# A hybrid decoder trunk on one core: branch gates computed one half branch ahead, and ScalarE's functions grouped by table

## The chip, the core and the metric

The kernel runs on one core of one Trainium2 chip. The metric is the device time of one launch in microseconds (us), lower is better. Engines are named as in the profile: PE is TensorE, DVE is VectorE, ACT is ScalarE, POOL is GpSimd, SP is SyncE, which here only issues DMAs.

## What is computed

Two layers of a decoder trunk act on 544 tokens (T: 512 of a prompt, 32 of eight sampled sequences), model width 1024, all in float32. A layer is, cut to what matters:

```
h = rmsnorm(x); p = h @ w_in            # columns for A, B, C, D and four gates of 1024 columns each
A: sparse attention                     # exp
B: retention, per-head norm; silu(g) * o          # rsqrt as exp(-0.5 ln), silu
C: HGRN2: silu(q), sigmoid(f), sigmoid(-f), ln, exp; per-head norm; silu(g) * o
D: Mamba-2: softplus(dt), exp, silu(conv); silu(z) * y; norm
up_b = branch_b @ w_branch[b]           # b = A, B, C, D
x = x + (sum_b sigmoid(gate_b) * up_b) @ w_out
x = x + (silu(rmsnorm(x) @ w_g) * (rmsnorm(x) @ w_u)) @ w_down
```

## The kernel before, in words

The residual x and the normed h lie transposed in SBUF for the whole run (`xT`, `hT`: 8 blocks of 128 channels by 544 tokens), and so do the four branch outputs (`brT`). Everything multiplied by a big weight is a **job**: a block of 512 weight columns, loaded by SP into one of two ring slots (`stream`), so that job j waits until job j-2 is finished on PE. `table` lists the products of all jobs in PE's order. A product of a gate is 128 columns by 272 tokens, 8 matmuls, and a gate job has 8 of them; a `wb` job (one half, 512 of 1024 columns, of a branch's projection) has 8 products of 4 matmuls. The trace records each of these float32 matmuls twice.

Product k goes into PSUM bank 6 + k%2, so PE may begin product k only when product k-2 has been taken out. ACT takes the gates (`take_act`: a copy per product into `sg`, and after the eighth one sigmoid over the whole half, 128 by 2176), and DVE takes the `wb` products (`take_dve`: times the gate, then added into `mg`). There is one `sg`, so DVE's first take of a `wb` job waits for the sigmoid of the gate job right ahead of it, and the next gate's first copy waits for the last take of the `wb` job before it.

The mixers B, C and D are chains over five token tiles (four of 128 tokens, one of 32) in which PE, ACT and DVE hand small matrices to each other. To fill PE's gaps the job products are dealt out among the chain's steps: `Share` holds the last job of a stage and a weight per gap, and at each `share.point` all three engines do their part of the products up to there. Every engine runs in program order, so a gate copy on ACT stands behind the chain's functions, and a `wb` take on DVE behind the chain's vector work. The stages are `stage_a` (A, with the jobs up to `dt`), `stage_retention` (gate00, wb00, gate01, wb01; the digits are branch and half), `stage_hgrn` (gates and wb of branch 1), `stage_ssm` (branch 2, in a part for the convolution and one for the scan), `stage_merge` (branch 3, then `wo`) and `stage_ff`.

The columns that B, C and D need (jobs r0 to r3, c0 to c3, z, xbc, dt) are copied by ACT out of PSUM into `stage` and sent to the DRAM buffers `spill`; the stages read them back tile by tile (L1438 for B, L1801 for C, L1960 for z). ACT applies silu to the tile when it is in: L1320 for B, L1597 and L1598 for C, L2070 for z. In B's stage SP does, from tile 2 on, in this order for each tile i: wait for the result of tile i-2 (`b_y`), load tile i, then load the next weights:

```
for i, (t0, m) in enumerate(tiles):
    if i >= 2:
        sp.wait_ge(S("b_y"), i - 1)
    sp.dma_start(inputs[0:m, i % 2], spill[0:4, ...]).then_inc(...)
    if i == 1: (load the states)
    if i >= 2:
        stream(sp, min(job0 + i - 1, job0 + 2), l)
```

ACT holds one set of function tables at a time. Where a function is not in the set that is loaded, an ACT_TABLE_LOAD stands ahead of it. The per-tile norm is ln and then exp (L1340 and L1341 in B, L1652 and L1653 in C, L2096 and L2097 in D) and each of the two gets a load of its own.

Of the kernel before, what the change touches and what calls it, by code (L numbers as in the profile page):

```python
# [53 lines left out]
def constants():  # L54
# [64 lines left out]
    for g in range(2):  # L119
# [8 lines left out]
HALF = T // 2  # L128

LAYER_SEMS = ("proj_ready", "taken_act", "taken_dve", "weights_in0", "weights_in1", "down_job_done", "dve_step", "act_step",  # L130
              "merged", "spilled0", "spilled1", "spilled2", "spilled3", "h_ready", "next_tile_in", "ret_stored", "hgrn_stored", "ssm_stored")


def trunk(nc, inp, out):

    es = ExitStack()
    with es:
# [46 lines left out]
        spill_dt = nc.dram_tensor("spill_dt", [T, 8], F32).ap()  # L184
        ps = [es.enter_context(nc.psum_tensor(f"ps{i}", [P, 512], F32)) for i in range(8)]
# [11 lines left out]
        sg = arena[:, AN - 4 * T:AN].rearrange("p (c t) -> p c t", c=4)  # L197
        merge_tmp = arena[:, AN - 5 * T:AN - 4 * T].rearrange("p (i t) -> p i t", i=2)
# [111 lines left out]
        for row in table:  # L310
            starts.append(starts[-1] + row[4])
        def in_strips(k):

            name, natural, at, _, _, _ = table[k]
            return natural and at == NT and jobs[J[name]][2] == 512
# [44 lines left out]
        def take_act(act, k):  # L360
# [27 lines left out]
            elif name[:4] == "gate":  # L388
                ins = act.activation(sg[:, at // P, t], bank[:, 0:HALF], ACT.Copy)  # L389
                if at == 3 * P and half == 1:  # L390
                    ach.link(act, ins)
                    ins = act.activation(sg[:, :, :], sg[:, :, :], ACT.Sigmoid)  # L392
            elif name[:2] == "gu":
                ins = act.activation(sg[:, at // P, t], bank[:, 0:HALF], ACT.Silu)  # L394
            else:
# [11 lines left out]
                else:  # L407
                    row = 8 if name == "z" else int(name[1]) + (4 if name[0] == "c" else 0)
                    if in_strips(k):
                        ins = act.activation(st[:, 0:P], bank[:, 0:P], ACT.Copy)  # L410
# [13 lines left out]
        def take_dve(dve, k):  # L424
# [7 lines left out]
            if name[:2] == "wb":  # L432
                n, db = jobs[J[name]][1]
                gate = max(i for i in range(k) if table[i][0][:4] == "gate")
                dve.wait_ge(S("taken_act"), taken_by(gate)[1])
                dst = mg[:, db * 4 + at // P, t]
                if n == 0:
                    dve.tensor_tensor(dst, bank[:, 0:HALF], sg[:, at // P, t], ALU.mult).then_inc(S("taken_dve"), 1)
                else:
                    tm = merge_tmp[:, k % 2, :]  # L440
                    dve.tensor_tensor(tm, bank[:, 0:HALF], sg[:, at // P, t], ALU.mult).then_inc(S("taken_dve"), 1)  # L441
# [28 lines left out]
        def take_to(who, eng, upto):  # L470
            for k in range(done[who], upto):
                if who == "act" and (table[k][0][:4] == "gate" or table[k][0][:2] == "gu") and table[k][5] == "act":

                    last = [i for i in range(k) if table[i][5] == "dve" and
                            (table[k][0][:4] == "gate" or table[i][0][:2] == "wo" or table[i][2] - 256 == table[k][2])]
# [121 lines left out]
        def rms_act(act):  # L597
            act.wait_ge(S("sq_summed"), 1)
# [25 lines left out]
        def stage_a(l):  # L624
# [140 lines left out]
            share = Share("r3", weights)  # L765
            with nc.Block() as block:
                @block.sync
                def _(sp):
                    stream(sp, J["r3"] + 3, l)
# [467 lines left out]
        def stage_retention(l):  # L1237
# [17 lines left out]
            job0 = J["gate01"]  # L1255
            with nc.Block() as block:
# [59 lines left out]
                def _(act):  # L1316
                    def gate(i):
                        m = tiles[i][1]
                        act.wait_ge(S(f"b_tile_in{i % 2}"), 16 * (i // 2 + 1))
                        act.activation(g(i)[0:m, :], g(i)[0:m, :], ACT.Silu).then_inc(S("b_inputs"), 1)  # L1320

# [5 lines left out]

                    share.point("act", act)
                    gate(0)
                    take_turned(0)  # L1330
                    for i, (t0, m) in enumerate(tiles):
                        share.point("act", act)
                        if i < 4:
                            gate(i + 1)
# [14 lines left out]
                def _(dve):  # L1349
# [25 lines left out]
                    for i, (t0, m) in enumerate(tiles):  # L1375
# [49 lines left out]
                        dve.wait_ge(S("b_inputs"), i + 1)  # L1425
# [6 lines left out]
                def _(sp):  # L1432
                    for w in range(4):
                        sp.wait_ge(S(f"spilled{w}"), 16 * 5)
# [12 lines left out]
                    for w in range(4):  # L1447
                        sp.wait_ge(S(f"spilled{w}"), 16 * 10)
# [8 lines left out]
        def stage_hgrn(l):  # L1457
# [28 lines left out]
            job0 = J["gate11"]  # L1486
            zbank = (0, 5)
            with nc.Block() as block:
# [98 lines left out]
                def _(act):  # L1587
                    def gates(i):
# [8 lines left out]
                        act.activation(q(i)[0:m, :], q(i)[0:m, :], ACT.Silu)  # L1597
                        act.activation(g(i)[0:m, :], g(i)[0:m, :], ACT.Silu).then_inc(S("c_inputs"), 1)  # L1598
# [65 lines left out]
                def _(dve):  # L1664
# [3 lines left out]
                    def forget(i):  # L1668
# [10 lines left out]
                        dve.wait_ge(S("c_inputs"), i + 1)  # L1679
# [134 lines left out]
        def stage_ssm(l):  # L1814
# [19 lines left out]
            with nc.Block() as block:  # L1834
# [35 lines left out]
                def _(act):  # L1870
# [4 lines left out]
                    ins.then_inc(S("conv_in_taken"), 1)  # L1875
                    act.wait_ge(S("dt_abs"), 1)
# [36 lines left out]
                def _(sp):  # L1913
                    for w in range(4):
                        sp.wait_ge(S(f"spilled{w}"), 16 * (17 if w < 2 else 16))
# [37 lines left out]
            job0 = J["gate21"]  # L1953
            with nc.Block() as block:
# [106 lines left out]
                def _(act):  # L2061
                    def take_front(i):
# [261 lines left out]
```

## Time and profile before

| | |
|---|---|
| device time, median of 3 runs (lowest, highest) | 4283.37 us (4275.71, 4287.13) |
| the profiled execution: device time | 4269.23 us |
| the profiled execution: span | 4267.4 us |
| PE busy | 3759.9 us, 88% |
| DVE busy | 1501.5 us, 35% |
| ACT busy | 859.2 us, 20% |
| mean granted clock of PE | 0.928 |

The span is cut by stage in the first layer as follows (the second layer is 2102.6 us later and the same): attention and the jobs up to `dt` to 806 us, B 812 to 979, C to 1247, D's convolution to 1318, D's scan to 1485, merge and `wo` to 1643, the feed-forward part to 2150. A busy time of PE is summed over instructions whose ends are modelled; time is lost where PE idles, and where the granted clock is below 1.00 (0.50 is 1.2 GHz, 1.00 is 2.4 GHz). A row "A <- B" says that A's engine was idle until B released it.

### The profile page before, as it was taken

To read this page: it belongs to the slowest core of one execution; us is meant where nothing else is said; L and a number is where in the kernel's file an instruction comes from. 1 tells how busy PE (TensorE), PEld (TensorE's weight loads), DVE (VectorE), ACT (ScalarE), POOL (GpSimd) and SP (SyncE) were. 2 spreads that over 40 slices of the span, in tenths; PEclk is the share of its full clock that TensorE was granted. 3 is DMA by queue.
4 is the path that set the end of the run, shared out by engine and by line. 5 is a ranking of instruction groups with operands and counts; after the bars stand their busy time and mean duration, and the time that the engine had idled before them with its cause. 6 is when DMAs were issued, how large, how long until landed. Compare 5 with 4: busy or idle time off the path is not lost. (4 is left out here: it accounts for less than half of the span.)

```text
span 4267.4 us, 43291 instructions
## 1 busy us (share of the span) xinstructions
PE 3759.9 (88%) x17542; PEld 2611.1 (61%) x17542; DVE 1501.5 (35%) x2591; ACT 859.2 (20%) x1674; POOL 198.4 (5%) x214
## 2 busy tenths in 40 slices
PE   5988899888878699999988889998788777999998
PEld 2543446666646477888845344566566564878887
DVE  2146393146745411000012555813476542110000
ACT  1122222124413210000012222222244141000000
POOL 0000411100000000000000013120000000000000
PEclk9988999799979799999999889998899788999999
DMA  3210454522121111212122124443211211212121
GB/s 99 71 61 33 147 170 131 180 76 70 45 72 61 53 69 60 79 60 74 55 67 82 38 69 161 167 164 133 83 57 35 72 61 49 72 60 79 60 74 56
DMA packets 254256, 352.57 MB, mean 83 GB/s; under 512 B 38142, under 2 KB 144254, under 8 KB 253924
## 3 DMA queue, kind: packets, MB, share of 16 engines
q1 hardware_dynamic: 213948, 249.67, 17.7%
q0 software_dynamic: 21504, 75.51, 5.3%
q10 hardware_dynamic: 18600, 24.55, 1.6%
q8 instruction: 142, 2.33, 0.2%
q14 instruction: 62, 0.51, 0.0%
HBM read 306.04 MB, written 43.66 MB: 82 GB/s over the span
## 5 line engine op out<-in xcount | busy, mean ns | idle before, releaser
L354 PE MATMUL ps<-hT,ring 128*128 128x272 f32 x5632 | 1391.2, 404 | 141.6 <-ACT arena L389 72.7
L354 PEld LDWEIGHTS ps<-hT,ring 128*128 128x128 f32 x5632 | 1083.4, 196 | 409.7 <-issue 98.3
L346 PE MATMUL ps<-ring,hT 128*128 128x512 f32 (+3 forms) x1728 | 718.8, 558 | 50.9 <-ACT stage L413 24.7
L346 PEld LDWEIGHTS ps<-ring,hT 128*128 128x128 f32 (+1 forms) x1728 | 305.8, 200 | 370.1 <-issue 335.7
L354 PE MATMUL ps<-branchT,ring 128*128 128x272 f32 x1024 | 289.4, 431 | 77.0 <-DVE arena L441 31.5
L2231 PE MATMUL ps<-arena,ring 128*128 128x272 f32 x1408 | 323.7, 393 | 3.0 <-DVE xT L2249 1.9
L2231 PEld LDWEIGHTS ps<-arena,ring 128*128 128x128 f32 x1408 | 267.2, 190 | 59.5 <-issue 2.7
L354 PEld LDWEIGHTS ps<-branchT,ring 128*128 128x128 f32 x1024 | 202.5, 206 | 154.6 <-DVE arena L441 40.8
L453 DVE TENSOR_TENSOR arena<-ps,arena 128x272 f32<-128x272 f32 x88 | 38.9, 442 | 602.0 <-PE ps L354 602.0
L394 ACT ACTIVATE arena<-ps 128x272 f32<-128x272 f32 x88 | 35.0, 397 | 586.6 <-PE ps L354 586.6
L910 DVE MAX8 branchT<-arena 32x8 f32<-32x2080 f32 x64 | 148.2, 2316 | 2.2
L911 DVE MATCH_REPLACE8 arena<-branchT,arena 32x2080 f32<-32x2080 f32 x64 | 147.0, 2297 | 0.0
L2249 DVE TENSOR_TENSOR xT<-xT,ps 128x272 f32<-128x272 f32 x32 | 11.5, 429 | 320.1 <-PE ps L2231 320.1
L441 DVE TENSOR_TENSOR arena<-ps,arena 128x272 f32<-128x272 f32 x96 | 42.1, 439 | 222.2 <-ACT arena L392 166.3
L354 PE MATMUL ps<-arena,ring 128*128 128x272 f32 x512 | 117.8, 393 | 2.2 <-issue 2.2
L354 PEld LDWEIGHTS ps<-arena,ring 128*128 128x128 f32 x512 | 97.1, 190 | 22.9 <-issue 3.0
L1149 ACT ACTIVATE branchT<-ps 128x512 f32<-128x512 f32 x128 | 69.5, 594 | 194.7 <-PE ps L1054 194.4
L389 ACT ACTIVATE arena<-ps 128x272 f32<-128x272 f32 x128 | 50.0, 391 | 254.8 <-PE ps L354 254.6
L801 PE MATMUL ps<-cst,arena 128*128 128x128 f32 x160 | 35.1, 324 | 52.0 <-ACT arena L852 51.7
L852 ACT ACTIVATE arena<-arena 128x128 f32<-128x128 f32 (+3 forms) x64 | 35.9, 561 | 204.7 <-DVE arena L893 204.7
L682 DVE TENSOR_TENSOR branchT<-arena 128x2560 f32<-128x2560 f32 (+1 forms) x4 | 8.6, 2154 | 190.8 <-PEq L643 190.8
L599 ACT ACT_TABLE_LOAD x4 | 5.1, 1283 | 337.9 <-issue 178.3
(384 smaller groups left out, 3810.1 us busy)
## 6 DMA issues: line engine op xcount, KB each, us to landing
ring<-in_w_in SPq DMA_DIRECT2D x44, 2048.0 KB, 8.3
ring<-in_w_gu SPq DMA_DIRECT2D x44, 1024.0 KB, 6.3
spill<-stage ACTq DMA_DIRECT2D x72, 256.0 KB
ring<-in_w_branch SPq DMA_DIRECT2D x16, 1024.0 KB, 5.0
arena<-spill SPq DMA_DIRECT2D x16, 1024.0 KB, 5.2
ring<-in_w_down SPq DMA_DIRECT2D x8, 2048.0 KB, 7.8
ring<-in_w_out SPq DMA_DIRECT2D x4, 2048.0 KB, 7.8
ring<-in_w_down SPq DMA_DIRECT2D x4, 1536.0 KB, 6.5
```

The lines of the kernel that those rows point to most:

```text
L346: mm = pe.matmul(bank[0:m, 0:w], hT[:, c, t0:t0 + m], slot3(j)[:, c, 0:w], start=(c == 0), stop=(c == kn - 1))
L354: mm = pe.matmul(bank[:, 0:HALF], slot3(j)[:, c, at:at + P], src, start=(c == 0), stop=(c == kn - 1))
L389: ins = act.activation(sg[:, at // P, t], bank[:, 0:HALF], ACT.Copy)
L394: ins = act.activation(sg[:, at // P, t], bank[:, 0:HALF], ACT.Silu)
L441: dve.tensor_tensor(tm, bank[:, 0:HALF], sg[:, at // P, t], ALU.mult).then_inc(S("taken_dve"), 1)
L453: dve.tensor_tensor(ff_ref[0][:, n, t], bank[:, 0:HALF], sg[:, (at - 256) // P, t], ALU.mult).then_inc(S("taken_dve"), 1)
L801: mm = pe.transpose(ps[2 + n % 2][:, s * P:s * P + P], Pr[:, n % 2, s * P:s * P + P], ident)
L852: act.activation(Pr[:, n % 2, 0:L], St[:, n % 2, 0:L], ACT.Exp, bias=mx[:, n % 2, 0:1], accum_out=sm[:, n % 2, 0:1]).then_inc(S("att_probs ...
L910: vch.link(dve, dve.max(m, src))
L911: vch.link(dve, dve.match_replace(work, m, src, TAKEN))
L1149: act.activation(KT[:, bb, j, :], ps[j][:, :], ACT.Copy).then_inc(S("kt_ready"), 1)
L2231: mm = pe.matmul(ps[2 * dc + half][:, 0:HALF], w, ff[:, fc, half * HALF:half * HALF + HALF], start=(fc == 0), stop=(fc == FC - 1))
```

## The change

Gates: there are now two gate buffers. Half 0 keeps `sg`; half 1 goes into `xT[:, 4:8]`, the upper half of the residual, which is stored to DRAM at the layer's start (`saved_x`) and loaded back in `stage_merge` before `wo1`. The jobs are reordered so that the gate of a half branch stands one `wb` job ahead: gate00, gate01, wb00, gate10, wb01, gate11, wb10, gate20, wb11 and so on to gate31, wb30, wb31. A gate's first copy waits for the `wb` job that used the same buffer last.

ACT: silu is applied in the copy out of PSUM for r3, c0, c3 and z, so the stages no longer apply it; the order of the projection jobs is changed so that these four stand together. `preload_act_table_set` names a set that has both ln and exp, at the head of the stages, after each gate sigmoid and after C's sigmoids.

```diff
-        jobs += [(f"r{i}", R_Q + 512 * i, 512) for i in range(4)]
-        jobs += [(f"c{i}", C_Q + 512 * i, 512) for i in range(4)]
-        jobs += [("z", M_Z, 512), ("xbc0", M_X, 512), ("xbc1", M_X + 512, 512), ("dt", M_DT, 8)]
+        jobs += [(f"r{i}", R_Q + 512 * i, 512) for i in range(3)] + [("c2", C_Q + 1024, 512), ("r3", R_Q + 1536, 512)]
+        jobs += [("c0", C_Q, 512), ("c3", C_Q + 1536, 512), ("z", M_Z, 512), ("c1", C_Q + 512, 512)]
+        jobs += [("xbc0", M_X, 512), ("xbc1", M_X + 512, 512), ("dt", M_DT, 8)]
         for n in range(4):
             for db in range(2):
-                jobs += [(f"gate{n}{db}", GATES + n * DM + db * 512, 512), (f"wb{n}{db}", (n, db), 512)]
+                if n == 0 and db == 0:
+                    jobs += [("gate00", GATES, 512)]
+                n2, d2 = n + db, 1 - db
+                if n2 < 4:
+                    jobs += [(f"gate{n2}{d2}", GATES + n2 * DM + d2 * 512, 512)]
+                jobs += [(f"wb{n}{db}", (n, db), 512)]
...
+        gates = (sg, xT[:, 4:8, :])
...
             elif name[:4] == "gate":
-                ins = act.activation(sg[:, at // P, t], bank[:, 0:HALF], ACT.Copy)
+                dst = gates[int(name[5])]
+                if name == "gate01" and at == 0 and half == 0:
+                    act.wait_ge(S("x_saved"), 16)
+                ins = act.activation(dst[:, at // P, t], bank[:, 0:HALF], ACT.Copy)
                 if at == 3 * P and half == 1:
                     ach.link(act, ins)
-                    ins = act.activation(sg[:, :, :], sg[:, :, :], ACT.Sigmoid)
+                    ins = act.activation(dst, dst, ACT.Sigmoid)
+                    ins.then_inc(S("taken_act"), 1)
+                    act.preload_act_table_set(LN_EXP)
+                    return
...
+                    fn = ACT.Silu if name in ("r3", "c0", "c3", "z") else ACT.Copy
...
-                        ins = act.activation(st[0:m, :], bank[0:m, :], ACT.Copy)
+                        ins = act.activation(st[0:m, :], bank[0:m, :], fn)
...
-                gate = max(i for i in range(k) if table[i][0][:4] == "gate")
-                dve.wait_ge(S("taken_act"), taken_by(gate)[1])
+                dve.wait_ge(S("taken_act"), taken_by(END[f"gate{n}{db}"] - 1)[1])
+                gate = gates[db][:, at // P, t]
...
+                if name == "wo1" and at == 0 and half == 0:
+                    dve.wait_ge(S("x_back"), 16)
...
         def rms_act(act):
+            act.preload_act_table_set("natural_log")
...
                     load_params(sp, l)
+                    sp.dma_start(saved_x, xT[:, 4:8, :]).then_inc(S("x_saved"), 16)
...
             share = Share("wb01", [6] + [1] * 25)
-            job0 = J["gate01"]
+            job0 = J["wb01"] - 1
...
-                    def gate(i):
-                        m = tiles[i][1]
-                        act.wait_ge(S(f"b_tile_in{i % 2}"), 16 * (i // 2 + 1))
-                        act.activation(g(i)[0:m, :], g(i)[0:m, :], ACT.Silu).then_inc(S("b_inputs"), 1)
...
+                    act.preload_act_table_set(LN_EXP)
...
-                        act.activation(q(i)[0:m, :], q(i)[0:m, :], ACT.Silu)
-                        act.activation(g(i)[0:m, :], g(i)[0:m, :], ACT.Silu).then_inc(S("c_inputs"), 1)
+                        act.preload_act_table_set(LN_EXP)
...
-                        act.wait_ge(S(f"z_in{i % 2}"), 16 * (i // 2 + 1))
-                        act.activation(z[0:m, i % 2, :], z[0:m, i % 2, :], ACT.Silu).then_inc(S("z_gate"), 1)
...
                 def _(sp):
+                    stream(sp, J["wo0"] + 1, l)
+                    sp.wait_ge(S("taken_dve"), taken_by(END["wb31"] - 1)[1])
+                    sp.dma_start(xT[:, 4:8, :], saved_x).then_inc(S("x_back"), 16)
                     stream(sp, J["wo1"] + 3, l)
```

The stage shares in products of matmuls change with the order of the jobs: B's stage now fills its gaps with three gates and two `wb` (256 matmuls, 192 before), `stage_merge` has one gate less, C and D have what they had.

How instructions move, first on **ACT in D's scan**, from the front of tile 1 (L2066 and L2084 are the same copy of the turned x, before and now) to the first gate copy behind it (L389, now L407). L2070 is the silu of z, L2096 and L2097 (now L2113, L2114) are the norm's ln and exp. Before:

```order
L2066 ACTIVATE arena<-ps 128x512
L2067 ACTIVATE arena<-ps 128x256
L2068 ACTIVATE arena<-ps 128x24
L2070 ACT_TABLE_LOAD
L2070 ACTIVATE arena<-arena 128x512
L2096 ACT_TABLE_LOAD
L2096 ACTIVATE arena<-arena,cst 128x2
L2097 ACT_TABLE_LOAD
L2097 ACTIVATE arena<-arena 128x2
L389 ACTIVATE arena<-ps 128x272
```

And now:

```order
L2084 ACTIVATE arena<-ps 128x512
L2085 ACTIVATE arena<-ps 128x256
L2086 ACTIVATE arena<-ps 128x24
L2113 ACTIVATE arena<-arena,cst 128x2
L2114 ACTIVATE arena<-arena 128x2
L407 ACTIVATE arena<-ps 128x272
```

Three table loads and the silu are gone from between the copies and the gate copy. In the whole program the loads are 148 before and 84 now.

Second, **PE in B's stage**, from the turning of tile 1 (L1264, now L1291) on. Matmuls with `hT` are a gate's, matmuls with `branchT,ring` are a `wb`'s; L1310 (now L1337) turns the result of tile 0, L1274 (now L1301) are tile 1's scores. Before:

```order
L1264 MATMUL ps<-cst,branchT 128x128 x8
L354 MATMUL ps<-hT,ring 128x272 x12
L1310 MATMUL ps<-cst,arena 128x128 x4
L354 MATMUL ps<-hT,ring 128x272 x2
L354 MATMUL ps<-branchT,ring 128x272 x10
L1274 MATMUL ps<-branchT 128x128 x4
L354 MATMUL ps<-branchT,ring 128x272 x7
```

And now:

```order
L1291 MATMUL ps<-cst,branchT 128x128 x8
L369 MATMUL ps<-hT,ring 128x272 x17
L1337 MATMUL ps<-cst,arena 128x128 x4
L369 MATMUL ps<-hT,ring 128x272 x16
L1301 MATMUL ps<-branchT 128x128 x4
L369 MATMUL ps<-hT,ring 128x272 x8
```

The gaps hold more work, and wb00 no longer follows gate00; it begins after tile 1's result is turned, behind gate01.

Third, **SP in B's stage**, from the load of tile 2 to the loads for C. L1438 (now L1457) loads a tile, L283 (now L293) is 2 MB of gate weights, L268 (now L278) 1 MB of `w_branch`. Before:

```order
L1438 DMA arena<-spill 128x4x512
L283 ISA
L283 DMA ring<-in_w_in 128x8x512
L1438 DMA arena<-spill 128x4x512
L268 ISA
L268 DMA ring<-in_w_branch 128x4x512
L1438 DMA arena<-spill 32x4x512
```

And now:

```order
L1457 DMA arena<-spill 128x4x512
L278 ISA
L278 DMA ring<-in_w_branch 128x4x512
L293 ISA
L293 DMA ring<-in_w_in 128x8x512
L1457 DMA arena<-spill 128x4x512
L278 ISA
L278 DMA ring<-in_w_branch 128x4x512
L1457 DMA arena<-spill 32x4x512
```

The weights between tile 2 and tile 3 are now wb00's and gate10's; the latter's slot is gate01's, so SP waits there until gate01 is finished on PE.

## Rows read from the trace of the kernel before

**Rows 1.** The page, busy time of PE and ACT.
```profile
PE 3759.9 (88%) x17542; PEld 2611.1 (61%) x17542; DVE 1501.5 (35%) x2591; ACT 859.2 (20%) x1674; POOL 198.4 (5%) x214
```

**Rows 2.** Waits of PE in B's stage: us in total, times, longest.
```profile
PE ps L354 <- DVE arena L438: 5.4, 5, 1.8
PE ps L354 <- ACT arena L392: 3.6, 2, 2.0
PE ps L354 <- ACT arena L389: 3.6, 3, 2.2
PE ps L1264 <- DVE arena L1371: 2.8, 2, 1.6
```

**Rows 3.** Waits of PE in C's stage.
```profile
PE ps L354 <- ACT arena L389: 12.5, 10, 3.3
...
PE ps L1503 <- DVE branchT L1687: 7.0, 2, 5.1
PE ps L354 <- ACT arena L392: 5.1, 2, 3.3
```

**Rows 4.** Waits of PE in D's convolution.
```profile
PE ps L354 <- ACT arena L389: 9.1, 1, 9.1
...
PE ps L354 <- ACT arena L392: 2.0, 1, 2.0
```

**Rows 5.** Waits of PE in D's scan.
```profile
PE ps L354 <- ACT arena L389: 13.0, 4, 5.1
...
PE ps L354 <- ACT arena L392: 1.6, 1, 1.6
```

**Rows 6.** Waits of PE in merge and `wo`.
```profile
PE ps L354 <- ACT arena L392: 2.8, 2, 2.0
```

**Rows 7.** Timeline of ACT at the last gate copy of gate30: start, us.
```profile
1519.07 1.28 ACT L392 ACT_TABLE_LOAD   x1
1520.37 2.02 ACT L392 ACTIVATE arena<-arena 128x2176 f32<-128x2176 f32 x1
```

**Rows 8.** Timeline of PE at the same place.
```profile
1522.43 13.10 PE L354 MATMUL ps<-branchT,ring 128*128 128x272 f32 x56 [2.04 <-ACT arena L392]
```

**Rows 9.** Timeline of ACT in D's scan, tile 1.
```profile
1340.09 1.28 ACT L2070 ACT_TABLE_LOAD   x1
...
1342.03 1.28 ACT L2096 ACT_TABLE_LOAD   x1
...
1343.63 1.28 ACT L2097 ACT_TABLE_LOAD   x1
...
1345.04 0.38 ACT L389 ACTIVATE arena<-ps 128x272 f32<-128x272 f32 x1
```

**Rows 10.** Timeline of DVE there: the sum that tile 0's norm waits for.
```profile
1341.07 0.69 DVE L2173 TENSOR_REDUCE arena<-arena 128x2 f32<-128x512 f32 x1
```

**Rows 11.** Windows: us, busy PE, PEld, DVE, ACT, POOL, PEclk, DMA share, GB/s.
```profile
1191.00:1198.00 7.00, 7.00 (x32) 4.12 (x31) 3.03 (x8) 1.56 (x2) 0.00 (x0) 0.51 0.00 0
1296.00:1303.00 7.00, 6.62 (x22) 5.20 (x23) 3.72 (x9) 2.36 (x4) 0.00 (x0) 0.76 0.52 197
1345.00:1352.00 7.00, 6.53 (x25) 5.40 (x26) 2.67 (x5) 1.02 (x3) 0.00 (x0) 0.54 0.14 37
```

**Rows 12.** DMA issues at the start of C's stage: count, KB, us to landing.
```profile
out_ret_sample<-arena SPq DMA_DIRECT2D x1, 2048.0 KB, 11.6
...
arena<-spill SPq DMA_DIRECT2D x1, 1024.0 KB, 12.2
```

**Rows 13.** DMA issue in B's stage, tile 2.
```profile
arena<-spill SPq DMA_DIRECT2D x1, 1024.0 KB, 4.5
```

**Rows 14.** Timeline of DVE in B's stage: scores taken, and the end of the rotation.
```profile
862.71 0.69 DVE L1379 TENSOR_TENSOR branchT<-ps,cst 128x512 f32<-128x512 f32 x1 [3.45 <-PE ps L1274]
...
869.25 0.69 DVE L1371 TENSOR_TENSOR branchT<-branchT,cst 128x512 f32<-128x512 f32 x1
```

**Rows 15.** Timeline of PE, merge: a gate job's 64 matmuls at full clock.
```profile
3637.98 29.50 PE L354 MATMUL ps<-hT,ring 128*128 128x272 f32 x128
```

More of the change, by code:

```diff
@@ L311, in trunk, with spilled_by @@
             starts.append(starts[-1] + row[4])
+        def spilled_by(name, w):
+            n = sum(1 for row in table[:END[name]] if row[0] not in ("aq", "akv", "iq", "ikiw"))
+            return 16 * len(range(w, n, 4))
         def in_strips(k):
@@ L408, in take_act @@
                     row = 8 if name == "z" else int(name[1]) + (4 if name[0] == "c" else 0)
+                    fn = ACT.Silu if name in ("r3", "c0", "c3", "z") else ACT.Copy
                     if in_strips(k):
-                        ins = act.activation(st[:, 0:P], bank[:, 0:P], ACT.Copy)
+                        ins = act.activation(st[:, 0:P], bank[:, 0:P], fn)
                         dst, src = (spill[row, t0:t0 + m, :].rearrange("t (x n) -> x t n", x=4), st[:, 0:P])
                     else:
-                        ins = act.activation(st[0:m, :], bank[0:m, :], ACT.Copy)
+                        ins = act.activation(st[0:m, :], bank[0:m, :], fn)
                         dst, src = (spill[row, t0:t0 + m, :], st[0:m, :])
@@ L433, in take_dve @@
                 n, db = jobs[J[name]][1]
-                gate = max(i for i in range(k) if table[i][0][:4] == "gate")
-                dve.wait_ge(S("taken_act"), taken_by(gate)[1])
+                dve.wait_ge(S("taken_act"), taken_by(END[f"gate{n}{db}"] - 1)[1])
+                gate = gates[db][:, at // P, t]
                 dst = mg[:, db * 4 + at // P, t]
                 if n == 0:
-                    dve.tensor_tensor(dst, bank[:, 0:HALF], sg[:, at // P, t], ALU.mult).then_inc(S("taken_dve"), 1)
+                    dve.tensor_tensor(dst, bank[:, 0:HALF], gate, ALU.mult).then_inc(S("taken_dve"), 1)
                 else:
                     tm = merge_tmp[:, k % 2, :]
-                    dve.tensor_tensor(tm, bank[:, 0:HALF], sg[:, at // P, t], ALU.mult).then_inc(S("taken_dve"), 1)
+                    dve.tensor_tensor(tm, bank[:, 0:HALF], gate, ALU.mult).then_inc(S("taken_dve"), 1)
                     dve.wait_ge(S("taken_dve"), taken_by(k)[1])
@@ L474, in take_to @@
                     last = [i for i in range(k) if table[i][5] == "dve" and
-                            (table[k][0][:4] == "gate" or table[i][0][:2] == "wo" or table[i][2] - 256 == table[k][2])]
+                            (table[k][0][:4] == "gate" and table[i][0][3:] == table[k][0][5:] or
+                             table[k][0][:2] == "gu" and (table[i][0][:2] == "wo" or table[i][2] - 256 == table[k][2]))]
                     if last:
@@ L764, in stage_a @@
                 weights += [1] * 8 + [(1, 18, 25, 34)[i]] + [1] * 18
-            share = Share("r3", weights)
+            share = Share("c2", weights)
             with nc.Block() as block:
@@ L768, in _ @@
                 def _(sp):
-                    stream(sp, J["r3"] + 3, l)
+                    stream(sp, J["c2"] + 3, l)
                 @block.tensor
@@ L1332, in _ @@
                         share.point("act", act)
-                        if i < 4:
-                            gate(i + 1)
                         share.point("act", act)
@@ L1433, in _ @@
                     for w in range(4):
-                        sp.wait_ge(S(f"spilled{w}"), 16 * 5)
+                        sp.wait_ge(S(f"spilled{w}"), spilled_by("r3", w))
                     for i, (t0, m) in enumerate(tiles):
@@ L1485, in stage_hgrn @@
             share = Share("wb11", weights)
-            job0 = J["gate11"]
+            job0 = J["wb11"] - 1
             zbank = (0, 5)
@@ L1678, in forget @@
                         dve.tensor_tensor(ki, ki, oml[0:m], ALU.mult)
-                        dve.wait_ge(S("c_inputs"), i + 1)
                         L(dve, dve.tensor_scalar(qi, qi, P ** -0.5, None, ALU.mult))
@@ L1875, in _ @@
                     ins.then_inc(S("conv_in_taken"), 1)
+                    act.preload_act_table_set(LN_EXP)
                     act.wait_ge(S("dt_abs"), 1)
@@ L1952, in stage_ssm @@
             share = Share("wb21", [1, 4] + [2, 2, 2, 2, 1] * 5)
-            job0 = J["gate21"]
+            job0 = J["wb21"] - 1
             with nc.Block() as block:
```

13 lines of the change are left out of this document (7 added, 6 removed).

## The prediction, made before the changed kernel ran

> **What bounds the kernel now.** I read the page first: PE is busy 3760 us of a span of 4267 us and ACT a fifth of it [rows 1]. So neither the 20% of ACT nor the number of its table loads is a time by itself. What counts is where PE idles and where its clock is low. The second view is PE's waits, cut by stage in the first layer; the second layer repeats it to a tenth, so every term below counts twice. Two releasers belong to this change. One is the sigmoid of a gate, L392: PE waits 3.6, 5.1, 2.0, 1.6 and 2.8 us for it in B, C, D's convolution, D's scan and merge [rows 2 to 6], 15.1 us a layer. The other is a gate's copy, L389, which on ACT stands behind chain functions and their table loads: 3.6, 12.5, 9.1 and 13.0 us [rows 2 to 5], 38.2 us a layer. The third view is the timeline. It shows why each wait is as long as it is, and so what part of it a shorter queue on ACT gives back. The fourth is the granted clock by window: after a wait of two or more us a window has 0.51 to 0.76, where it is 1.00 in undisturbed ones [rows 11]. A stall is paid again in matmuls at 1.2 GHz.
>
> **The sigmoid leaves the path.** After a gate's last copy ACT loads a table (1.28 us) and runs the sigmoid (2.02 us) [rows 7]; PE gets through two `wb` products and then waits 2.04 us [rows 8]. Now the `wb` behind a gate uses the sigmoid of the gate before, and a gate job of 29.5 us [rows 15] or a `wb` job lies between. All 15.1 us go.
>
> **Fewer table loads and no silu ahead of the gate copies.** The sets loaded fall from 148 to 84, 64 times 1.28 us, or 82 us of ACT. Only what is left of a wait counts:
> - D's scan. In tile 1 ACT loads for silu from 1340.09, loads for ln from 1342.03, for exp from 1343.63, and copies the gate at 1345.04 [rows 9]. DVE's sum for the norm is ready at 1341.76 [rows 10]. Without loads and silu, ln, exp and copy follow that, and the copy starts about 2.7 us sooner. In the next two tiles the sum comes last and only the load between ln and exp goes: 1.3 us each. With 0.2 at a small wait: 5.5 of the 13.0 us.
> - C. At each change of tile one load goes between ln and exp (1.28), and load plus silus give way to one preload ahead of the first gate copy, 1.07 us sooner. Capped by the single waits that stand there, this is 5.5 of the 12.5 us. At the stage's start, the longest wait for L1687 (5.1 us) shortens by 1.05, since ln then starts when DVE has its input and not when the load ends, and the second, at tile 4, by about 0.8: 1.8 us of 7.0.
> - D's convolution. One load (1.3 us) goes from the chain ahead of its gate copy, the rest of the 9.1 us is DMA and DVE. A silu load comes twice in a row with a preload after gate21's sigmoid; nothing on PE waits for it, and if something did it would be 1.3 us.
> - B. The three gate-copy waits are 3.6 us. But ACT now runs gate00's sigmoid, with a load on both sides (4.6 us), between the turn of tile 1 and the norm of tile 0. Walking the new order puts the norm's end behind it and leaves PE a wait of 1.0 us; 2.6 us go.
>
> The Trainium skill, page "ScalarE: Activation LUTs", section "What ACT_TABLE_LOAD costs", puts a drain of about 1.4 us beside each load of 1283 ns, 2.66 us in all. In the rows the load is 1.28 us and the next instruction starts 0.02 us behind it, so the trace does not agree; by the page, the nine or so loads priced above would give some 12 us a layer more.
>
> **B's stage is laid out anew.** Its gaps hold 256 matmuls for 192. In three tiles PE comes to the turn of the next tile later by one or two of them (0.46 us each), while DVE's rotation takes the time it took: of the 4.9 us for L1371, 2.8 of it in [rows 2], 1.9 go. The 5.4 us for DVE's takes of wb00 (L438) are those behind a rotation on DVE; with wb00 in another place I take 1.8 off. Against this a new wait. SP loads tile 3 only behind gate10's weights, and those only once gate01 is finished on PE (T). 2 MB and then 1 MB go out; before, a tile alone lands in 4.5 us [rows 13], and one put behind 2 MB in 12.2 [rows 12]. So tile 3 is in at T+12.6, the rotation of about 6 us (6.6 from scores to its end [rows 14]) ends at T+18.6, while PE, with wb00's first part, the scores and the next gap, is at the turn at T+13.3: a wait of 5.3 us. Its bounds are 0, if the tile lands as one alone does, and 12 if nothing covers it. I take 5.3, since the nearest row has exactly this order. B gives 3.6 + 2.6 + 1.9 + 1.8 - 5.3 = 4.6 us a layer.
>
> **The clock.** Three windows behind waits that vanish had 0.51, 0.76 and 0.54 over 7 us [rows 11]: at 1.00 they give back 3.4 us (C, behind a wait of 3.3 for the sigmoid), 1.7 (convolution) and 3.2 (scan). In B one such dip goes and one comes with the new wait. The bounds are 0 and these values; I take them whole, as each has the wait right ahead of it.
>
> **Edits at nothing.** Silu in the copy out of PSUM costs 0.63 us for 0.60 on an ACT that is mostly idle there. The store of half of x (1.1 MB) goes behind the parameters and ahead of weights that PE needs 30 us later. Its load back starts when wb31 is taken and has wo0, 29 us, before DVE needs it; wo1's 2 MB behind it (7.9 us alone) still make it. If that cover were gone, some 5 us would show per layer. The merge stage loses a gate that B has gained; the matmuls are the same in sum.
>
> **Sum.** Per layer B 4.6; C 5.1 + 5.5 + 1.8 + 3.4 = 15.8; convolution 2.0 + 1.3 + 1.7 = 5.0; scan 1.6 + 5.5 + 3.2 = 10.3; merge 2.8: 38.5 us, twice 77. The profiled execution of 4269 would be 4192. It lies 14 us below the median of the runs; against that median, 4283.4, the forecast is 4206 us, 1.8% faster. About 0.3%, 13 us, can be told from no change.
>
> **Rivals.**
> 1. *The waits for ACT turn into waits for DVE.* In B and D's scan the `wb` takes stand behind DVE's chain work (L438 in [rows 2]), and what ACT no longer delays meets that. Only the sigmoid's 15.1 us and the clock behind it stay, less the 5.3: some 16 us a layer, 4251. For it: in two scan tiles DVE's sum was the last already. Against it: C's and tile 1's loads end last in the timeline. Chance 0.17.
> 2. *The shorter queue gives more.* Tile 3 lands in time (+5.3), gate copies lose most of their waits (20 more us of 38.2 than I took, less the convolution's DMA part, so about 12), and PE keeps its clock through the scan (some 3): 20 us a layer more, 4166. For it: waits come in rows, and one that goes moves the next. Chance 0.13.
> 3. *A load costs more than its row.* If a drain stood beside each load in a place the rows don't show, some 12 us a layer come on top: 4182. The Trainium skill's page on ScalarE, named above, is its source. The gap of 0.02 us speaks against it. Chance 0.03.
> 4. *SP's queue in B decides, and the kernel is slower.* SP is blocked on gate01 and again on wb00; tiles 3 and 4 come late. Unhidden, this is at most 12 us, then 8 for the smaller tile 4, and two dips of 3.4, near 28 a layer. The gains without the new wait are 43.8, so it decides only where it comes with rival 1: 15 to 20 of gain against 28 is some 10 us a layer on the other side, 4303. It makes the kernel slower from the point where the loss passes what ACT gives back. Chance 0.04.
> 5. *It doesn't do what it says.* The loads are moved, not removed, or the chain's pace is DVE's and PE's everywhere: within 13 us of before. The order of instructions shows 64 loads less, which speaks against it. Chance 0.04.
>
> **The numbers.** The forecast has 0.59, with 4185 to 4230 as its own range. From 4166 to 4251 takes in rivals 1 and 2 at their values and the bounds of the clock and of the new wait; I give 4165 to 4253. Faster by over 0.3%: 0.59 + 0.17 + 0.13 + 0.03 = 0.92, same 0.04, slower 0.04.
>
> **What would show it.** PE's waits for the sigmoid line gone in all five stages. In D's scan tile 1, the gate copy within 1.5 us of DVE's sum. A wait of 4 to 7 us at the turn of tile 3 in B, with DVE waiting for the tile's DMA. Windows behind the old waits at 1.00. B's stage longer by a gate less 5 us, about 25, and merge shorter by about 32. Wrong, if the waits for ACT fall and those for DVE in the same stage rise by as much, or if `wo1` waits for x.

## The result, and the profile after

The changed kernel takes 4247.2 us (median of 4 runs, 4243.9 to 4252.2), the kernel before, run beside it, 4285.3 us (4275.7 to 4297.6): a ratio of 0.9909, 95% interval 0.989 to 0.9928, so 0.9% faster. The forecast was 1.8%, 4206 us with 4253 as its upper end. The gain between the medians, 38 us, is half of the 77 us of the sum. Between the two profiled executions it is 25 us, since the one of the kernel before, 4269 us, lies 14 us below the median of its runs.

The page of the profile after, span and busy time:

```profile
span 4242.1 us, 43167 instructions
...
PE 3764.1 (89%) x17542; PEld 2619.8 (62%) x17542; DVE 1501.7 (35%) x2591; ACT 754.9 (18%) x1570; POOL 198.6 (5%) x214
```

ACT lost 104 us of work [rows 1] and the span 25 us. PE's busy time did not fall (3759.9 before). So whatever was gained between these two executions was gained in PE's waits, both layers together (us in total, times, longest):

```profile
PE ps L369 <- DVE arena L463: 31.0, 16, 4.7
...
PE ps L369 <- ACT xT L407: 23.8, 10, 7.9
PE ps L369 <- ACT arena L407: 23.4, 16, 3.8
PE ps L369 <- ACT arena L410: 18.1, 8, 3.4
PE ps L361 <- DVE hT L613: 18.0, 2, 9.1
PE ps L369 <- ACT xT L410: 17.9, 8, 2.9
```

The same view of the kernel before (L389 is now L407, the gate's copy; L392 is now L410, its sigmoid):

```profile
PE ps L354 <- ACT arena L389: 76.5, 36, 9.1
...
PE ps L354 <- DVE arena L441: 33.9, 16, 4.7
PE ps L354 <- ACT arena L392: 30.5, 16, 3.3
```

The waits for copies fell from 76.5 to 47.2 us, by 29.3. The waits for the sigmoid, which the change was to take off the path, did not fall but rose from 30.5 to 36.0, still 16 times, once for each gate job. By stage of the first layer they are 6.1, 6.2, 2.0, 1.6 and 2.0 us, against 3.6, 5.1, 2.0, 1.6 and 2.8 [rows 2 to 6]. Two things are behind the rise. B's stage now has three gate jobs and merge one, where each had two. And in the kernel before the sigmoid of gate31 found its tables still in, so L392 has 14 loads for 16 sigmoids and PE waited 0.76 us there; now each sigmoid has its load (L410 has 16), and the wait in merge is 2.04 us.

The timelines of PE and ACT in the changed kernel show why, at the end of a gate job in the merge stage:

```profile
1532.73 1.77 PE L369 MATMUL ps<-hT,ring 128*128 128x272 f32 x7
1534.34 2.00 PE L369 MATMUL ps<-branchT,ring 128*128 128x272 f32 x8
1538.38 6.91 PE L369 MATMUL ps<-branchT,ring 128*128 128x272 f32 x29 [2.04 <-ACT xT L410]
```

```profile
1534.60 0.40 ACT L407 ACTIVATE xT<-ps 128x272 f32<-128x272 f32 x1 [3.27 <-PE ps L369]
1535.01 1.28 ACT L410 ACT_TABLE_LOAD   x1
1536.31 2.02 ACT L410 ACTIVATE xT<-xT 128x2176 f32<-128x2176 f32 x1
1538.34 1.28 ACT L412 ACT_TABLE_LOAD   x1
```

The sigmoid writes `xT`, a gate that no product needs for a whole job. The copy of the eighth product has emptied its PSUM bank at 1535.0. PE runs one `wb` product and waits 2.04 us all the same, until the sigmoid ends at 1538.34. `product` lets PE write a bank when `taken_act` has reached `taken_by(k - 2)`, and for a gate's eighth product that count is given not by the copy but by the sigmoid behind it. On this reading PE waits for the bank, not for the gate, and the second gate buffer does nothing about a bank. Run e1 tests it.

### The profile page after: what moved, and what is told of

It reads as the page before. It is cut to its first block and busy times, and to the rows that moved or that the text cites. A ratio compares the mean times of both kernels' runs of the same rounds, so it can differ in the third digit from the quotient of the medians.

```text
span 4242.1 us, 43167 instructions
## 1 busy us (share of the span) xinstructions
PE 3764.1 (89%) x17542; PEld 2619.8 (62%) x17542; DVE 1501.7 (35%) x2591; ACT 754.9 (18%) x1570; POOL 198.6 (5%) x214
## 5 line engine op out<-in xcount | busy, mean ns | idle before, releaser
L477 DVE TENSOR_TENSOR arena<-ps,arena 128x272 f32<-128x272 f32 x88 | 38.9, 442 | 603.7 <-PE ps L369 603.7
L415 ACT ACTIVATE arena<-ps 128x272 f32<-128x272 f32 x88 | 35.0, 398 | 586.6 <-PE ps L369 586.6
L828 PE MATMUL ps<-cst,arena 128*128 128x128 f32 x160 | 35.1, 324 | 52.1 <-ACT arena L879 51.8
L619 PE MATMUL ps<-hT,cst 128*128 128x272 f32 x128 | 39.0, 476 | 37.6 <-DVE hT L606 37.6
L828 PEld LDWEIGHTS ps<-cst,arena 128*128 128x128 f32 x160 | 20.9, 160 | 79.3 <-issue 73.2
```

The source lines that it names most:

```text
L477: dve.tensor_tensor(ff_ref[0][:, n, t], bank[:, 0:HALF], sg[:, (at - 256) // P, t], ALU.mult).then_inc(S("taken_dve"), 1)
L619: mm = pe.matmul(ps[half][:, 0:HALF], ones, hT[:, c, half * HALF:half * HALF + HALF], start=(c == 0), stop=(c == KC - 1))
L828: mm = pe.transpose(ps[2 + n % 2][:, s * P:s * P + P], Pr[:, n % 2, s * P:s * P + P], ident)
```

## The experiments

All ratios are to the kernel before, run on the same chip at the same time; the runs were made on several chips, so where two versions did not run side by side the ratios are the safer comparison. G stands for gates ahead (second buffer, store and reload of x), T for the tables' part (silu at the copy out of PSUM, job order, preloads), R for the bank released at the copy.

### e1: the bank is free at the copy (G, T, R)

```diff
                 if at == 3 * P and half == 1:
-                    ach.link(act, ins)
-                    ins = act.activation(dst, dst, ACT.Sigmoid)
                     ins.then_inc(S("taken_act"), 1)
+                    act.wait_ge(S("taken_act"), taken_by(k)[1])
+                    act.activation(dst, dst, ACT.Sigmoid).then_inc(S("gated"), 1)
...
-                dve.wait_ge(S("taken_act"), taken_by(END[f"gate{n}{db}"] - 1)[1])
+                dve.wait_ge(S("gated"), sum(1 for x in jobs[:J[f"gate{n}{db}"] + 1] if x[0][:4] == "gate"))
```

> The changed kernel, with the bank of a gate job's eighth product counted as free at its copy instead of at the sigmoid behind it; DVE's products with the gates wait for a count of their own that the sigmoid gives. Theory A (the sigmoid kept its place on PE's path only through that count: 36.0 us of PE's waits in 16 places): those waits go to under 4 us, the kernel takes 26 to 38 us less than the changed one, 4209 to 4221 us, ratio to the kernel before 0.982 to 0.985. Rival B (the count is a label only: ScalarE has load and sigmoid, 3.3 us, to do in any case, and PE waits for the next thing ScalarE owes it, the chain's copies in the retention and hgrn stages): the waits move to the lines of the chains' copies and the ratio stays at 0.989 to 0.992.

Measured: 4220.0 us, ratio 0.9851 (0.9834 to 0.9868), 27 us below the changed kernel. PE's waits in e1:

```profile
PE ps L369 <- DVE arena L463: 39.5, 18, 4.7
...
PE ps L369 <- ACT xT L407: 24.8, 12, 7.9
...
PE ps L369 <- ACT arena L407: 23.4, 16, 3.8
```

No line of the sigmoid (now L411) is left, 36.0 us of waits are gone. The waits for VectorE's products took 8.5 us of it back, those at the turn in B some 3.8, those for the copies 1.0. At the place shown above PE now runs from the gate job into `wb` without a stop, while ACT does the same load and sigmoid beside it:

```profile
1495.07 32.12 PE L369 MATMUL ps<-hT,ring 128*128 128x272 f32 x128 [12.57 <-PEq L156]
1527.02 29.50 PE L369 MATMUL ps<-branchT,ring 128*128 128x272 f32 x128
```

Theory A holds (the time is at the slow end of its range), rival B falls.

### e2: the same release in the kernel before (R alone)

Same edit, with `sg` as the one buffer.

> The kernel before, its gate order and its one buffer kept, with the same one edit: the eighth copy frees the bank, the sigmoid has a count of its own. It tells what gating ahead is worth once the bank is freed early. Theory A: PE then waits only at the third product of the wb job, whose bank DVE frees after the sigmoid: copy 0.5, load 1.3, sigmoid 2.0 and DVE 0.45 against two products of 1.84 leave 0.5 to 0.7 us where 2.04 stood, 16 times, so 20 to 26 us less than before, ratio 0.994 to 0.9955. Rival B (what PE needs is the gate itself, so only a gate computed ahead can hide it): under 6 us less, ratio 0.9985 to 1.0.

Measured: 4264.6 us, ratio 0.995 (0.9932 to 0.9968), 20 us less. PE at gate30, the place of [rows 8]:

```profile
1515.79 3.83 PE L354 MATMUL ps<-branchT,ring 128*128 128x272 f32 x16
1520.39 11.27 PE L354 MATMUL ps<-branchT,ring 128*128 128x272 f32 x48 [0.76 <-DVE arena L442]
```

Without any gate ahead, 2.04 us became 0.76: the wait is now for DVE, which waits for the sigmoid, and it comes behind two products instead of one. Of the price put on the sigmoid, most was the price of the bank.

### e3 and e4: the two halves of the change

> The changed kernel with its gate jobs in the old order and one gate buffer (no store and reload of x), its tables, silus and job order kept. Theory A (the gates ahead bought nearly nothing): the time of the changed kernel within 8 us, ratio 0.990 to 0.993. Rival C (gates ahead paid about half, by freeing the copies from waiting for VectorE): ratio 0.995 to 0.996.

> The kernel before with the gates one half branch ahead, the second buffer and the store and reload of x, and nothing of the tables. Theory A: within 10 us of the kernel before, ratio 0.998 to 1.0. Rival C: 19 us less, ratio 0.995 to 0.996. Rival D (the reload of x and the gate weights ahead on the queue cost something that the tables' gain hides): slower, ratio 1.001 to 1.004.

Measured: T alone 4259.2 us, 0.9935 (0.9919 to 0.9951); G alone 4281.2 us, 0.9988 (0.9977 to 0.9999). T alone has the copies' waits at 51.1 us and the sigmoid's at 35.1. G alone leaves the sigmoid's at 33.9 (18.1 and 15.8). So about two thirds of the change's 38 us are the tables' part (26 us), and the other part gives 3.6 us alone and 12 on top of T. e3 lies between the two ratios that were expected, nearer A's, 12 us above the changed kernel where A had 8.

### e7 and e8: the square with R closed

> Tables, silus and job order of the change, old gate order and one gate buffer, and the bank freed at the eighth copy. With e1, e3 and the changed kernel it closes the square. Theory A (gating ahead is worth something only where the bank is freed early: it then hides the sigmoid from VectorE's first product, which e2 showed as 9.3 us of waits, and VectorE's part in the copies' waits): 8 to 22 us above e1, 4228 to 4242 us, ratio 0.987 to 0.990. Rival E (the early release alone does it, gates ahead are worth nothing in any setting): within 5 us of e1, ratio 0.985 to 0.986.

> The kernel before with the gates ahead and the bank freed at the eighth copy, and nothing of the tables. Theory A: the 34 us of waits for the sigmoid that the gates alone left are gone, and the tables' loads between them stay: 4281 less 24 to 34 is 4247 to 4257 us, ratio 0.991 to 0.9935. Rival F (without the tables' part ScalarE is too full, and the waits move to its copies): ratio 0.995 to 0.998.

Measured: T and R 4222.0 us, 0.9865 (0.9845 to 0.9885), within 2 us of e1, where I had expected 8 to 22 more; but the two ran on different chips. G and R 4244.6 us, 0.9915 (0.9899 to 0.9931), the ratio as expected, the time 2 us below its range. e1 and e7 once more, side by side:

> e1 once more, on one chip with its rival: early release and gates ahead. If gates ahead are worth nothing once the bank is freed early (what e7 against e1 showed across two chips), its time is within 5 us of the next run's; if they are worth the 8.7 us of waits by which the two traces differ, it is 8 us less.

> e7 once more, on one chip with e1: early release, tables, old gate order, one buffer, no store and reload. As above: within 5 us of e1 if gates ahead are worth nothing, 8 us more if the traces' difference in waits is what counts.

e1 again: 4212.8 us, 0.9836 (0.9822 to 0.985); e7 again: 4221.3 us, 0.9855 (0.9836 to 0.9873). Here gates ahead show 8.5 us. The traces differ by as much in waits: in e7 the copies' are 51.1 and VectorE's products' 45.3, in e1 48.2 and 39.5.

### e5 and e6: tile 3 ahead of the weights

```diff
-                        if i >= 2:
+                        if i >= 3:
                             stream(sp, min(job0 + i - 1, job0 + 2), l)
```

> e1 with one thing more: in the retention stage SyncE issues tile 3's load ahead of the weights of the second branch's first gate job instead of behind them. In e1 tile 3's rotation came late and PE waited 3.3 us for it, in the changed kernel 1.4. If the 2 MB ahead of it on the queue are the cause, that wait goes, 2 to 7 us over both layers, ratio to before 0.9835 to 0.9848. If the tile is late because its buffer comes free late, the wait stays and the time is e1's within 2 us. The weights come at most 6 us later and have some 20 us to spare.

> The changed kernel with tile 3's load ahead of the same weights. The forecast put 5.3 us per layer on that place, the trace shows 1.4, as PE comes to the tile later. Theory A: 0 to 3 us less over both layers, ratio 0.990 to 0.991. If the forecast's price was right and only shown elsewhere: 8 to 10 us less, ratio 0.9885 to 0.989.

Measured: e5 4221.6 us, 0.9864 (0.9844 to 0.9883); e6 4247.7 us, 0.9924 (0.9907 to 0.9941). Nothing gained, in either. B's stage in e5, PE's waits:

```profile
PE ps L369 <- DMA ring<-in_w_branch: 3.2, 1, 3.2
PE ps L1291 <- DVE arena L1391: 2.6, 2, 1.4
```

The tile lands in 5.8 us for 11.3 and the longest wait for a tile's turn fell from 3.3 to 1.4 us, but PE now waits 3.2 us at the start of `wb00`. In e6 the same two waits are 1.4 and 2.7 us. The edit does more than its words: with `i >= 3` the whole call at tile 2 falls away, and that call loads wb00's weights as well as gate10's. SyncE's issues in e1 and then in e5:

```profile
866.31 0.37 SPq L278 DMA_DIRECT2D ring<-in_w_branch  x1
892.90 0.37 SPq L293 DMA_DIRECT2D ring<-in_w_in  x1
893.31 0.58 SPq L1457 DMA_DIRECT2D arena<-spill  x1
```

```profile
863.02 22.05 SPq L1457 DMA_DIRECT2D arena<-spill  x2
885.25 0.38 SPq L278 DMA_DIRECT2D ring<-in_w_branch  x1
890.16 0.38 SPq L293 DMA_DIRECT2D ring<-in_w_in  x1
```

The `arena<-spill` of e5 stands for two loads, tile 2's and, 22 us later, tile 3's. The `ring<-in_w_branch` in both is wb00's: issued at 866 us in e1, at 885 in e5, where PE is ready for it at 890. I had counted spare time for gate10's weights and not for wb00's, which went with them. So the runs show that 2 MB ahead of the tile are why it lands late, and they don't show what the right order (wb00's weights, tile 3, gate10's weights) would give: that was not run.

### e9 and e10: why the copies are late

In e7 the longest wait for a copy is 7.9 us, in D's convolution. ACT idles for 7.5 us right ahead of that wait, for the convolution's inputs, with a finished product in its bank, and has its own steps to do before it comes to the copy.

```diff
                     share.point("act", act)
+                    take_to("act", act, done["act"] + 2)
                     act.wait_ge(S("conv_in_turned"), 1)
```

> e7 with one line more: in the convolution ScalarE copies out the two products that TensorE has already finished before it starts to wait for the convolution's inputs. There PE waited 7.9 us per layer for a copy. Theory: ScalarE was not busy but late by its place in the order, so the wait goes and 10 to 16 us over two layers with it: 4206 to 4212, ratio 0.9825 to 0.984. Rival G: the waits for DVE's convolution steps behind it take over: within 4 us of e7.

Measured: 4226.4 us, 0.9866 (0.985 to 0.9882), no gain. PE in e9 runs two products on and then waits as long:

```profile
1260.87 7.60 PE L362 MATMUL ps<-hT,ring 128*128 128x272 f32 x32
1275.91 10.11 PE L362 MATMUL ps<-hT,ring 128*128 128x272 f32 x32 [7.44 <-ACT arena L398]
```

A copy given early once is no help where each later point of the stage is again one product behind. `fill_to` finds the product k that PE began last before the point and calls `take_to` with `k - 1`; the range there excludes its end, so the last product taken is k-2, and k-1, which is finished, stays in its bank until the next point. e10 changes the rule itself, for ACT:

```diff
-            take_to(who, eng, k - 1)
+            take_to(who, eng, k if who == "act" else k - 1)
```

"Every finished product" below means every one up to k-1.

> e7 with ScalarE's rule changed everywhere: at each point of a stage it copies out every product TensorE has finished, not all but the last. Theory: the copies' waits, 51.1 us in e7, fall by 20 to 35, 4187 to 4202 us, ratio 0.978 to 0.982. Rival H: ScalarE now stands waiting for a product that is not done while its chain step could run, and VectorE's and the chains' waits rise by as much: 4215 to 4235.

Measured: 4179.3 us, 0.9755 (0.9741 to 0.977), 42 us below e7 run beside it (e12) and 104 below the kernel before. PE's waits in e10:

```profile
PE ps L362 <- DVE arena L454: 44.9, 24, 4.7
...
PE ps L1509 <- DVE branchT L1691: 22.8, 8, 4.8
...
PE ps L2056 <- DVE arena L2184: 18.1, 6, 4.1
...
PE ps L362 <- ACT arena L398: 8.1, 2, 4.1
```

The copies' waits are 8.1 for 51.1 us, and those for spilled projections (L426) 9.0 for 24.7. Part came back at DVE: L1691 (C's logarithms) rose from 13.6, L2184 (the end of the scan's norm) from 1.8, L1715 in C from 4.9 to 10.9.

### e13 to e16: what each part is worth with early copies

> e10 with the gates ahead and the second buffer: e1 with ScalarE copying out every finished product. e1 and e7 left the worth of gates ahead between 0 and 9 us. If gates ahead are worth VectorE's waits for the sigmoid also here (9 us in the traces, less the clock): 4165 to 4175 us, ratio 0.973 to 0.975. If they are worth nothing: 4176 to 4184, ratio 0.9755 to 0.977.

> The kernel before with the early release and ScalarE copying out every finished product, nothing of the change itself. It tells what the tables' part is worth once the copies are not late for another reason. The tables' part gained by making late copies less late (29.3 us of the copies' waits); theory: most of that lateness is now gone in another way, so it is worth 8 to 20 us here instead of 38, 4190 to 4200 us, ratio 0.978 to 0.981. Rival: the table loads stand on the chain itself and keep their full price: 4214 to 4220 us, ratio 0.984 to 0.986.

> e10 with VectorE too taking every finished product. PE still waits 44.9 us for VectorE's products with the gates. VectorE is the chains' own engine, with little time between its steps, so standing for a product costs the chain: expected between 10 us less and 10 us more than e10, 4170 to 4190 us, ratio 0.974 to 0.978.

> The changed kernel with ScalarE copying out every finished product, the eighth bank still freed by the sigmoid. If the two causes are separate, late copies and late release, they add: the copies' waits go (some 40 us) and the sigmoid's 36 us stay: 4203 to 4212 us, ratio 0.981 to 0.983. If they are one, the sigmoid's waits go too: 4170 to 4180.

Measured: e13 (G, T, R) 4171.0 us, 0.9755 (0.9736 to 0.9774). e14 (R, no change) 4201.8 us, 0.9821 (0.9801 to 0.9841): without T the kernel is 22 us above e10, or 0.66% by the ratios. With late copies T was worth 0.85% (e2 against e7), so it keeps more than half of its worth. The expectations (4190 to 4200, or 4214 and more) had it a little too cheap. In e14 the wait that is larger than in e10 above all is the one for DVE's step behind ACT's norm in the scan, 26.2 us for 18.1: there a load stands between ln and exp on the chain itself (1.28 us, at 1336.34 us in e14), ahead of the step that PE waits for. e15 4181.3 us, 0.9771 (0.975 to 0.9791), no different from e10: waits for DVE's products fell from 44.9 to 31.3, and the chain's rose from 18.1 to 25.8 among others. e16 (G, T, the bank still freed by the sigmoid) 4189.5 us, 0.979 (0.9773 to 0.9808), 58 us below the changed kernel (1.2% by the ratios) where some 40 were expected. Its sigmoid waits are 22.7 us for 36.0: late copies and late release are two causes, but they meet. My reading, which I did not follow up in the rows, is that a copy that starts sooner lets its sigmoid end sooner.

The last pair put e10 and e13 on one chip:

> e10 once more, beside e13 on one chip. Gates ahead worth nothing: both within 4 us. Gates ahead worth VectorE's waits for the sigmoid: e13 is 6 to 10 us less.

> e13 once more, beside e10 on one chip: 4167 to 4175 us if gates ahead are worth 6 to 10 us, within 4 us of e10 if nothing.

e10 again: 4182.9 us, 0.9767 (0.9749 to 0.9785); e13 again: 4178.3 us, 0.9755 (0.9736 to 0.9775). G against no G in seven comparisons of medians, in the order of the runs: 3.6, 12, 20, 2, 8.5, 8.3 and 4.6 us. Four of the seven are between runs that were not side by side (the second, third, fourth and sixth), and by the ratios, which take the chip out, the seven are 0.12, 0.26, 0.35, 0.14, 0.19, 0.00 and 0.12%. Never a loss, on average 0.17% or some 7 us, but most pairs by themselves can hardly be told from nothing. I take gates ahead as worth a few us, 4 to 9 by the three pairs that ran side by side; the size is not settled.

The fastest version by its medians is e13: the change with a bank freed at its copy and ACT copying every finished product, 4171 and 4178 us. e10, without the second buffer and the 4.5 MB of traffic for it, has medians 5 to 8 us higher; by the ratios it is level in one pair and 0.12% behind in the other.

## Why the prediction was half right

**The copies: right.** The sum took off 29.8 us (twice 2.6, 5.5, 1.3 and 5.5), the rows show 29.3, and stage by stage 3.6, 4.4, 1.2 and 5.4 in the first layer. In the scan the gate copy follows at once on exp, with no load between ln, exp and copy:

```profile
1364.56 0.30 ACT L2113 ACTIVATE arena<-arena,cst 128x2 f32<-128x2 f32 x1 [1.72 <-DVE arena L2190]
1364.88 0.20 ACT L2114 ACTIVATE arena<-arena 128x2 f32<-128x2 f32 x1
1364.99 0.38 ACT L407 ACTIVATE arena<-ps 128x272 f32<-128x272 f32 x1
```

DVE's sum, L2190, ends at 1364.52, and the copy starts 0.5 us later, where 1.5 was the mark. B did better (its copies' waits are gone) and C less well (8.1 us left of 12.5).

**The sigmoid: wrong, and it is the step that failed.** The step reads "PE gets through two `wb` products and then waits 2.04 us" and ends "All 15.1 us go". Two readings in it were not made. The first is a count. [rows 15] shows a gate job's 64 matmuls as x128, so a matmul leaves two records there; in [rows 8] the stretch behind the wait is x56, 28 matmuls, seven of the eight products of four. One product had run, not two. A wait at the second product is for the bank of the gate's eighth; one for the gate, through DVE, can only come at the third, since DVE must have emptied the first `wb` bank by then, and e2 shows it there, 0.76 us long. The second is the code: the releaser named in a row, L392, is whoever raises the count, and one count had two meanings, bank free and gate ready. The change separated them in memory and not in the count. Cost of the step: 30.2 us forecast, -5.5 measured. In e1, where the bank is released at the copy, 36.0 us of waits go and the time falls by 27 us.

**The clock: right in place, wrong in sum.** The sum had 16.6 us from three low windows that would rise to 1.00. Two of them (C and convolution) stood behind a sigmoid's wait, and that wait stayed. The third (scan) stood behind a copy's wait, and that one went. The same three places in the changed kernel (columns as in [rows 11]):

```profile
1213.50:1220.50 7.00, 7.00 (x33) 4.28 (x32) 3.03 (x8) 0.86 (x2) 0.00 (x0) 0.53 0.00 0
1318.50:1325.50 7.00, 6.92 (x23) 5.45 (x24) 3.77 (x9) 3.35 (x5) 0.00 (x0) 0.76 0.47 180
1366.00:1373.00 7.00, 6.12 (x38) 5.34 (x38) 3.57 (x7) 1.97 (x4) 0.00 (x0) 1.00 0.15 37
```

Where the wait is gone the clock is at 1.00, and in e1, where the other two waits go as well, all three places have 1.00. But low stretches come up in other places. The scan's first 7 us had 0.63 in the kernel before and have 0.50 in the changed kernel:

```profile
1341.00:1348.00 7.00, 6.88 (x24) 6.09 (x25) 2.51 (x4) 2.24 (x4) 0.00 (x0) 0.50 0.93 260
```

In sum nothing is left of the term: PE's busy time went from 3759.9 to 3764.1 us, and the four runs have a mean clock of 0.923 to 0.926, where the kernel before had 0.921 to 0.929. What the sum left out is that a stretch of low clock that goes in one place can come back in another. Of the versions with T and R and without gates ahead, e7, e9, e10, e12 and e17 have a mean clock 0.001 to 0.0035 above the kernel before beside them, e15 one 0.001 below it. And in all seven pairs above the version with gates ahead has the lower mean clock, by 0.0003 to 0.004, though most of that is within what one kernel does from run to run. No run shows why.

**B's layout and SyncE's queue: the late tile is there, the wait for it is not.** Tile 3 does go out behind 2 MB and lands in 11.1 us, where I had 12.2. PE waits for its rotation:

```profile
906.04 1.09 PE L1291 MATMUL ps<-cst,branchT 128*128 128x128 f32 x8 [1.42 <-DVE arena L1391]
```

It waits 1.4 us and not 5.3, since PE came later too: ahead of it stand 1.99 us for the sigmoid and 1.13 for VectorE (L460). And these 1.4 us are not the tile's: it is in at 899.5, DVE takes a `wb` product at 899.69 and starts the rotation at 900.05, and in e6, where the tile is in early, the wait is 1.42 as well. With the sigmoid's wait gone, in e1, it is 3.3, and there DVE does wait for the tile's DMA, 1.78 us; e5, with the tile early, has 1.4 again. For DVE's steps in B and C the sum had 11.0 us of gain less 10.6 for this new wait, both layers, 0.4 in all; they came to some 4.5: L1687's waits fell by 1.5, the turn's, with the new wait in them, by about 3.7, L438's rose by 0.7. Waits not in the sum gave 7: 4.4 less at the start of a layer (L588 in the kernel before, 22.4; in e7 and its repeat e12 this wait is 22.2 and 20.0 us, so half of it can be chance) and 2.9 at L441.

**Together:** the measured rows give -5.5 for the sigmoid, 29.3 for copies, -4.2 for busy PE, 4.5 for B's and C's steps and 7.3 beside the sum: 31 us, against 25 between the two spans. Of the 6 us between, 3.1 are a new wait in attention (L1039, for a copy of ACT at L1160) and 1.8 one in the scan (L2069, for DVE's L2197); the rest lies in waits too small to be followed. Rival 1 came nearest in time, 4251, but for another reason, so that is luck: it kept the sigmoid's gain and lost the copies', while it was the other way round. Rival 3 is not borne out: in the rows of ACT above, load and sigmoid, and sigmoid and load, follow each other within 0.02 us, and nothing like a drain shows; T alone gave 26 us, where the terms for the copies, worked out without a drain, had 29.8. Store and reload of x cost nothing that shows: the reload lands in 5.5 us and no wait for it is in the trace.

## What to carry to other kernels

A wait is named by the instruction that raised the semaphore, and that says neither what was waited for nor that a second buffer would end it. Ask which products ran between the last release and the wait: that tells the resource. Where one count stands for two things (bank empty, result ready), split the count first; here that was a handful of lines and worth 18 to 37 us in five comparisons of medians, gates ahead 2 to 20 us in seven. And when an engine that is 20% busy is late, look for its place in the written order before its load. With the bank released early and one gate buffer, one product's lag in the rule of taking cost 1.3% without T and 1.1% with it, the tables' part (64 loads and the silus) 0.85% with the lag and 0.66% without.

## What the runs showed of the hardware

The time of one and the same program goes with its granted clock: over 54 runs of the kernel before, the 7 at a mean clock of 0.923 took 4289.8 us, the 13 at 0.925 took 4283.9 and the 3 at 0.928 took 4273.0, some 3 us for 0.001. A profile taken at 0.928, as that of the kernel before was, comes from a run some 10 us below the median of its kernel, as much as some of the terms that were argued from it. Why a run has one value or the other is open.
